# Output products split in two and new engine orders in the RWKV-7 stage of a two-block model on one core

## The reference, cut to what matters

```
def step(state, inp):                       # per head; state is 64 x 64
    r_t, w_t, k_t, v_t, kk_t, a_t = inp
    sa = einsum("bhvk,bhk->bhv", state, -kk_t)
    state = state * w_t + sa * (kk_t * a_t) + v_t * k_t
    y = einsum("bhvk,bhk->bhv", state, r_t)
# then, per head: y = (y - mean(y)) * rsqrt(var(y) + eps); * lnx_w + lnx_b; + bonus; * g
```

## Time and profile before

| | |
|---|---|
| median of three runs | 1938.07 us |
| profiled execution, its own time | 1937.32 us |
| its span, first to last instruction | 1935.4 us |
| PE busy | 1908.9 us, 99% |
| PE weight loads (PEld) busy | 1646.4 us, 85% |
| DVE (VectorE) busy | 1356.2 us, 70% |
| ACT (ScalarE) busy | 847.8 us, 44% |
| mean granted TensorE clock | 0.998 |

### The profile page before, as it was taken

The page is one execution under the profiler, slowest core; times in us unless marked ns, Lnnn a source line. Parts: engine busy times, 40 slices in busy tenths (PEclk is TensorE's granted clock), DMA queues, the critical chain, the costliest instruction groups (busy, mean ns, idle before and its releaser), DMA issues.

```text
span 1935.4 us, 31929 instructions
## 1 busy us (share of the span) xinstructions
PE 1908.9 (99%) x13562; PEld 1646.4 (85%) x13562; DVE 1356.2 (70%) x1796; ACT 847.8 (44%) x1272; POOL 120.9 (6%) x130
## 2 busy tenths in 40 slices
PE   8999999999999999999999999999999999999998
PEld 7877897888788898887989889889887778898897
DVE  7776868576677777667545687767677768777665
ACT  5443744354354334344224454434445645334342
POOL 0155100000000000010000000000002300000000
PEclk9999999999999999999999999999999999999999
DMA  7322402237123233224220132323342113233231
GB/s 241 119 66 66 137 9 90 77 132 131 44 96 101 92 105 110 88 86 135 88 87 23 65 105 94 108 88 109 109 138 87 50 50 103 93 104 110 87 109 45
DMA packets 138829, 182.58 MB, mean 94 GB/s; under 512 B 4917, under 2 KB 103429, under 8 KB 138304
## 3 DMA queue, kind: packets, MB, share of 16 engines
q1 hardware_dynamic: 135392, 168.91, 26.7%
q0 software_dynamic: 3296, 11.63, 2.9%
HBM read 172.66 MB, written 7.34 MB: 93 GB/s over the span
## 4 chain that ended last, share of the span: by engine, by line
PE 94%; DVE 3%; ACT 1%; issue 1%; DMA 0%; DVEq 0%; ACTq 0%
PE X L1680 21%; PE M L1592 19%; PE M L1593 19%; PE M L1594 18%; PE X L713 2%; PE M L1653 1%; PE M L1655 1%; PE M L1654 1%; PE M L2015 1%; PE X L1992 1%; PE X L2003 1%; PE X L1870 1%; DVE w_lo L2519 1%; PE X L1832 0%; PE M L700 0%
## 5 line engine op out<-in xcount | busy, mean ns | idle before, releaser
L1593 PE MATMUL M<-u,raw_lo 128*128 128x512 f32 x728 | 287.9, 396 | 0.0
L1592 PE MATMUL M<-u,w_hi 128*128 128x512 f32 x728 | 287.9, 395 | 0.0
L1594 PE MATMUL M<-u,w_hi 128*128 128x512 f32 x728 | 286.1, 393 | 0.0
L2170 ACT ACTIVATE us<-X 128x256 f32<-128x256 f32 x160 | 61.7, 386 | 433.3 <-PE X L1680 433.2
L2111 ACT ACTIVATE w_hi<-raw 128x2048 fp32r<-128x2048 f32 x111 | 211.7, 1907 | 76.4 <-PE M L1594 42.9
L2677 DVE TENSOR_TENSOR h<-h,M 128x512 f32<-128x512 f32 x184 | 123.6, 684 | 144.9 <-PE M L1594 144.7
L1680 PE MATMUL X<-t,w_hi 128*128 128x256 f32 x936 | 173.2, 282 | 0.0
L1594 PEld LDWEIGHTS M<-u,w_hi 128*128 128x128 f32 x728 | 137.7, 189 | 32.9
L1592 PEld LDWEIGHTS M<-u,w_hi 128*128 128x128 f32 x728 | 136.8, 188 | 30.8
L1593 PEld LDWEIGHTS M<-u,raw_lo 128*128 128x128 f32 x728 | 136.7, 188 | 29.8
L2519 DVE TENSOR_TENSOR raw_lo<-raw,w_hi 128x2048 fp32r<-128x2048 f32 x57 | 130.3, 2286 | 23.7 <-ACT w_hi L2111 23.7
(11 more groups left out here) (561 smaller groups left out, 4581.9 us busy)
## 6 DMA issues: line engine op xcount, KB each, us to landing
raw<-in_w_up_dram SPq DMA_DIRECT2D x48, 1024.0 KB, 5.3
raw<-in_w_down_dram SPq DMA_DIRECT2D x48, 1024.0 KB, 5.1
raw<-in_w_in_dram SPq DMA_DIRECT2D x12, 1024.0 KB, 7.3
raw<-in_a_w_in_dram SPq DMA_DIRECT2D x12, 1024.0 KB, 5.2
h<-in_x_dram SPq DMA_DIRECT2D x16, 256.0 KB, 4.1
raw<-in_w_mk_dram SPq DMA_DIRECT2D x4, 1024.0 KB, 5.1
raw<-in_w_mv_dram SPq DMA_DIRECT2D x4, 1024.0 KB, 5.3
raw<-in_w_out_dram SPq DMA_DIRECT2D x4, 1024.0 KB, 5.1
```

The costliest lines, as they stand in the source:

```text
L1592: mm(dst, wh, xh, start=start, stop=False)
L1593: mm(dst, wl, xh, start=False, stop=False)
L1594: return mm(dst, wh, xl, start=False, stop=stop)
L2170: nc.scalar.activation(at_, region(n, r), ACT.Copy).then_inc(S["st_snap"], 1)
```

## The change

The output operation is divided: `YA` holds the 64 records inside the chunks, `Y` the 28 records with the states. The wait between the parts becomes a wait for `YA`'s own count, and other operations now stand between the two. `half_done` and its semaphore go. For pairs 1 and 3 the output uses banks 2 and 3 in place of banks 0 and 1. The three lists get new orders, and some operations get other banks. The number and shapes of all instructions stay the same.

```
-RW_QUAD = ("L", "RBT", "AR", "PQ", "WG", "MR", "N", "Y")
+RW_QUAD = ("L", "RBT", "AR", "PQ", "WG", "MR", "N", "YA")
 RW_PE = """...
-    TT6.0.1 Z2.1.2 X.1.3 WG.0.2 TT6.1.0 MR.0.1 WG.1.2 N.0.0 fill.25 S1.0.0 MR.1.1 S2.0.1 N.1.2 S3.0.0 S1.1.1 S4.0.0 S2.1.1
-    fill.26 S5.0.0 S3.1.1 fill.27 S6.0.0 S4.1.1 kk2.3.2 S5.1.0 Y.0.2 S6.1.0
-    Y.1.0 var.0.2 var.1.3 fill.28 tV.2.2 fill.29 fill.30 bonus.2.2 fill.31 gate.0.3 gate.1.0 fill.32 tV.3.1 fill.33 fill.34
-    tKd.2.1 L.2.2 fill.35 tBd.2.1 fill.36 RBT.2.1 P2.2.1 PT2.2.0 AR.2.2 P4.2.1 PQ.2.1 L.3.2 TT3.2.0 P8.2.1
-    tA.2.2 fill.37 tBd.3.0 bonus.3.3 tA.3.0 fill.38 tKd.3.0 fill.39 TT4.2.0 P2.3.1 PT2.3.2 Z.2.0 RBT.3.2 P4.3.1 PQ.3.1
+    TT6.0.1 Z2.1.2 X.1.3 WG.0.2 TT6.1.0 MR.0.1 WG.1.2 N.0.0 MR.1.1 N.1.2 S1.0.0 fill.25 S2.0.0 S1.1.1 fill.26 S3.0.0 S2.1.1
+    fill.27 S4.0.0 S3.1.1 YA.0.2 S5.0.0 S4.1.1 YA.1.1 S6.0.0 S5.1.1 fill.28 S6.1.1 Y.0.2 Y.1.1
+    var.0.1 kk2.3.0 var.1.1 tV.2.1 fill.29 fill.30 bonus.2.4 fill.31 gate.0.0 gate.1.1 fill.32 tV.3.3 fill.33 fill.34
+    tKd.2.3 L.2.2 fill.35 tBd.2.3 fill.36 RBT.2.1 P2.2.1 PT2.2.0 AR.2.2 P4.2.1 PQ.2.1 L.3.2 P8.2.1
+    tA.2.0 TT3.2.2 fill.37 tBd.3.0 bonus.3.3 tA.3.0 fill.38 tKd.3.0 fill.39 TT4.2.0 P2.3.1 PT2.3.2 Z.2.0 RBT.3.2 P4.3.1 PQ.3.1
...
-    MR.2.1 WG.3.2 N.2.0 fill.41 S1.2.0 MR.3.1 S2.2.1 N.3.2 S3.2.0 S1.3.1 S4.2.0 S2.3.1 fill.42 S5.2.0 S3.3.1
-    S6.2.0 S4.3.1 fill.43 S5.3.0 Y.2.1 S6.3.0 fill.44 var.2.0 fill.45 Y.3.0 gate.2.2 var.3.3 fill.46 fill.47 gate.3.2""".split()
+    MR.2.1 WG.3.2 N.2.0 MR.3.1 N.3.2 S1.2.0 fill.41 S2.2.0 S1.3.1 fill.42 S3.2.0 S2.3.1 YA.2.2 S4.2.0 S3.3.1
+    YA.3.1 S5.2.0 S4.3.1 fill.43 S6.2.0 S5.3.1 fill.44 S6.3.1 Y.2.2 Y.3.1 var.2.0 fill.45 gate.2.1 var.3.0 fill.46 fill.47 gate.3.1""".split()
 RW_ACT = """...
-    PT4.1 P8.0 P8.1 sq.3 Z.0 Z.1 Z2.0 X.0 yd.0 Z2.1 tA.1 X.1 W.0 G.0 W.1 N.0 G.1 yd.1 yd.2 N.1 yd.3 w.7 dsq.0 ln.3 dsq.1 rn.3
-    var.0 grs.0 tV.2 var.1 ex.3 neg.2 grs.1 ex.2 inc.2 inc.3 dc.3 tV.3 dec.2 dc.2 tKd.2 neg.3 w.8 tBd.2 dec.3 P2.2 PT2.2 P4.2
+    PT4.1 P8.0 P8.1 sq.3 Z.0 Z.1 Z2.0 X.0 yd.0 Z2.1 tA.1 X.1 W.0 G.0 W.1 G.1 N.0 N.1 yd.1 yd.2 yd.3 w.7 dsq.0 dsq.1 ln.3 rn.3
+    var.0 grs.0 var.1 tV.2 ex.3 neg.2 grs.1 ex.2 inc.2 inc.3 dc.3 tV.3 dec.2 dc.2 tKd.2 neg.3 w.8 tBd.2 dec.3 P2.2 PT2.2 P4.2
...
-    dsq.2 var.2 grs.2 dsq.3 var.3 yr.2 grs.3 w.10 yr.3""".split()
+    dsq.2 dsq.3 var.2 grs.2 var.3 yr.2 grs.3 w.10 yr.3""".split()
 RW_DVE = """...
-    TT6.1 MT.0 RT.0 yd.0 S1.0 S2.0 MT.1 S3.0 RT.1 S1.1 S4.0 S2.1 S5.0 yd.1 S3.1 S6.0 yd.2 S4.1 S5.1 S6.1 w.7 kk2.3 t.2 ev.12
+    TT6.1 MT.0 RT.0 yd.0 MT.1 S1.0 RT.1 S2.0 S1.1 S3.0 S2.1 ev.12 S4.0 S3.1 S5.0 S4.1 S6.0 S5.1 yd.1 S6.1 w.7 yd.2 kk2.3 t.2
...
-    K.2 ev.15 B.2 kmod.3 Kd.2 ev.16 R.2 yc.1 bonus.2 Bd.2 L.2 PT.2 gate.1 RBT.2 A.3 B.3 K.3 RKT.2 Kd.3 rk.3 AKT.2 TT2.2 ev.17
-    Bd.3 TT3.2 L.3 R.3 w.8 PT.3 TT4.2 T4.2 ev.18 ev.19 RBT.3 bonus.3 TT2.3 yr.0 TT5.2 T5.2 TT3.3 AKT.3 TT4.3 TT6.2 T4.3 RKT.3
-    TT5.3 T5.3 TT6.3 MT.2 RT.2 S1.2 S2.2 MT.3 S3.2 RT.3 S1.3 S4.2 S2.3 S5.2 S3.3 S6.2 S4.3 w.9 ev.20 S5.3 S6.3 var.2 yb.2 yc.2
+    K.2 ev.15 B.2 kmod.3 Kd.2 ev.16 bonus.2 R.2 yc.1 Bd.2 L.2 PT.2 gate.1 RBT.2 A.3 B.3 K.3 RKT.2 AKT.2 Kd.3 rk.3 TT2.2 ev.17
+    Bd.3 TT3.2 L.3 R.3 w.8 PT.3 TT4.2 T4.2 bonus.3 ev.18 ev.19 RBT.3 TT2.3 yr.0 TT5.2 T5.2 TT3.3 AKT.3 TT4.3 TT6.2 T4.3 RKT.3
+    TT5.3 T5.3 TT6.3 MT.2 RT.2 MT.3 S1.2 RT.3 S2.2 S1.3 S3.2 S2.3 S4.2 S3.3 S5.2 S4.3 S6.2 S5.3 w.9 ev.20 S6.3 var.2 yb.2 yc.2
...
-        RW_BANKS[_x] = RW_QUAD_SETS[_b] if _x[0] in RW_QUAD else (_b,)
+        RW_BANKS[_x] = RW_BANKS[("YA", _x[1])] if _x[0] == "Y" else RW_QUAD_SETS[_b] if _x[0] in RW_QUAD else (_b,)
...
-    if st == "Y":
+    if st == "YA":
         return [("d", ("var", hp))]
...
     for x in RW_OPS["p"]:
-        if x[0] != "fill":
+        if x[0] == "Y":
+            after[x] = []
+        elif x[0] != "fill":
...
-                         S1=["a.N", "d.MT"], Y=["d.S6", "d.RT", "d.RKT", "a.G"], gate=[], var=["a.dsq"])
+                         S1=["a.N", "d.MT"], YA=["d.RKT", "a.G"], Y=["d.S6", "d.RT"], gate=[], var=["a.dsq"])
...
-                    half_done(last)
+                else:
+                    wait("rw_mm", RW_NO["p"][("YA", hp)])
```

More of the change, by code:

```diff
@@ L187 @@
-    var.0 grs.0 tV.2 var.1 ex.3 neg.2 grs.1 ex.2 inc.2 inc.3 dc.3 tV.3 dec.2 dc.2 tKd.2 neg.3 w.8 tBd.2 dec.3 P2.2 PT2.2 P4.2
-    PT4.2 P8.2 tA.2 tBd.3 tA.3 yr.0 tKd.3 w.9 P2.3 PT2.3 Z.2 P4.3 PT4.3 yr.1 P8.3 Z2.2 X.3 Z.3 X.2 Z2.3 W.2 G.2 W.3 N.2 G.3 N.3
-    dsq.2 var.2 grs.2 dsq.3 var.3 yr.2 grs.3 w.10 yr.3""".split()
+    PT4.1 P8.0 P8.1 sq.3 Z.0 Z.1 Z2.0 X.0 yd.0 Z2.1 tA.1 X.1 W.0 G.0 W.1 G.1 N.0 N.1 yd.1 yd.2 yd.3 w.7 dsq.0 dsq.1 ln.3 rn.3
+    var.0 grs.0 var.1 tV.2 ex.3 neg.2 grs.1 ex.2 inc.2 inc.3 dc.3 tV.3 dec.2 dc.2 tKd.2 neg.3 w.8 tBd.2 dec.3 P2.2 PT2.2 P4.2
@@ L190 @@
+    PT4.2 P8.2 tA.2 tBd.3 tA.3 yr.0 tKd.3 w.9 P2.3 PT2.3 Z.2 P4.3 PT4.3 yr.1 P8.3 Z2.2 X.3 Z.3 X.2 Z2.3 W.2 G.2 W.3 G.3 N.2 N.3
+    dsq.2 dsq.3 var.2 grs.2 var.3 yr.2 grs.3 w.10 yr.3""".split()
 RW_DVE = """cs.0 dl.0 cs.1 t.0 ev.4 t.1 kmod.0 w.2 dl.1 ev.5 csx.0 csx.1 dn.0 kk2.0 kmod.1 w.3 ev.6 kk.0 beta.0 Kd.0 K.0 rk.0 Bd.0 ev.7 Kd.1
@@ L256, in program @@
             da_sq da_ss da_ln da_rstd da_y
-            rw_shift rw_p rw_lora rw_act rw_dve rw_half rw_mm y_hi y_lo
+            rw_shift rw_p rw_lora rw_act rw_dve rw_mm y_hi y_lo
             ms_hi ms_lo ma_score ma_max ma_neg ma_exp ma_rz ma_p ma_tr ma_pt_hi ma_pt_lo ma_pv ma_hi ma_lo
@@ L627, in operand @@
                 return blk(sl(name, hp), hh, cp, cpar)
[L629 to L635, removed]
             def out_of_psum(st, hp):
@@ L718, in rwkv_pe @@
                                   start=True, stop=True)
-                elif st != "Y":
+                elif st == "N":
                     for cp in range(4):
@@ L726, in rwkv_pe @@
                                 last = mm(o_, tmv(2, hp, hh, cp, cpar), tmv(3, hp, hh, cp, cpar), start=False, stop=True)
-                else:
+                elif st == "YA":
                     for cp in range(4):
```

## The result

The changed kernel takes 1944.03 us (median of 7 runs, 1942.56 to 1945.71); the kernel before, beside it, 1938.17 (1937.30 to 1938.66). The ratio is 1.003, 95% interval 1.0019 to 1.0042: 5.9 us slower. The profiled execution is the slowest of the seven, 1945.71 us; its span of 1943.9 is 8.5 us above that of before. Part of this is no effect of the change: `N.0`, the first operation behind which the new order begins, starts at 276.01 us in place of 274.44, because TensorE's first matmul came 0.5 us later and about 1 us more was lost before 76 us of the span. I therefore measure one stretch in every profile, from the start of `N.0` to the second matmul of the output projection behind the lists: 109.3 us before (274.44 to 383.76), 116.3 us after (276.01 to 392.27), so 6.9 more. The lines of the changed kernel are numbered 5 or 6 lower than those of before.

The account below looks back on a forecast made before the run. TensorE, busy 99%, was taken as the bound, with only 6.6 us of its waits at stake. Savings and added waits over six steps summed to +1.6 us on the median of 1938.07, so 1939.7 us, range 1936.9 to 1942.3.

Parts of the forecast that it names:

- Step 2: First stand: var.1 in its new bank waits for ScalarE 2.9 us, then tV.2 0.85; 3.7 us added.
- Step 5: States of pairs 2 and 3: 2.0 us saved, then 3.2 added as fill.44 waits for VectorE (second stand).
- rival (a): TensorE's clock falls behind the stands: 1941.3 us for one fall, 1942.9 for two; chance 0.20.
- Step 1: Pairs 0 and 1, up to var.0: waits at state steps, var and inside Y go, about 2.2 us saved.
- Step 3: Gates: gate.1 moves to a free bank and no longer waits for VectorE, 0.9 to 1.0 us saved.
- Step 4: Pairs 2 and 3 before their states: PQ.3 starts 0.4 to 0.5 us earlier, whatever happened before; 0.4 saved.
- Step 6: Tail: fill.46 waits 0.95 us for the bank that ev.21 empties; 0.8 us added.
- Rival (b): Stands smaller than read, TensorE runs into VectorE at L.2 and PQ.3: 1935.4 to 1937.5 us; chance 0.10.
- Rival (c): A wait priced at zero among the P, TT and Z products: 1940.5 to 1941.5 us; chance 0.10.

Follow-up runs that it names:

- e8: Changed kernel with both long TensorE waits mended and VectorE's yd.1, yd.2, w.7 moved into gaps, then the 3.1 us wait at fill.44 put back: 1940.04 us.
- e9: Same as e8, but w.9 and ev.20 two steps earlier on VectorE, so the wait at fill.44 is 1.2 us: 1936.20 us.
- e4: As e1, with w.9 and ev.20 moved two steps earlier on VectorE to shorten the wait at fill.44: 1938.89 us.
- e1: Changed kernel with kk2.3 earlier on TensorE and VectorE, var.1 in bank 0, ScalarE's var.0 ahead of rn.3, removing the first stand: 1942.49 us.
- e2: Changed kernel with VectorE's ev.20 ahead of S4.2 and w.9 behind S6.3, removing the second stand at fill.44: 1939.25 us.
- e3: Changed kernel with the mends of e1 and e2 together, and VectorE's ev.21 ahead of w.9 and var.2: 1936.92 us.
- e6: Kernel before with only the output divided into YA and Y, old orders and old banks: 1937.64 us.
- e5: As e2, plus ScalarE's var.0 ahead of ln.3 and rn.3; banks and TensorE's order as in the changed kernel: 1937.16 us.

## Why the prediction was wrong

The predicted 1939.7 us and the upper end of 1942.3 both lie below 1944.03.

The step that failed is the price of the two stands: steps 2 and 5 charge their length alone, and the sum puts what the clock does behind them at nothing. The falls stand only in rival (a), at a chance of 0.20, and two of them at 0.10, with 1.5 to 1.9 us for each. The profile shows both falls, and the mean clock of 0.995 or 0.996 says the same of all 7 executions. They are worth, by rows of the changed profile: 1.0 us more in `var.1`, 1.0 in `tV.2` and 0.6 to 0.7 in the first seven matmuls of `fill.29`, 2.6 in all, for the first; and for the second 1.7 us, half of the 3.4 us at the low level, all of them work (378.4 to 381.8 us). Between e8 and e9 the part of the 3.8 that isn't length is 1.9 us. Even rival (a) with two falls, 1942.9, would have been 1.1 us too low: a second term that the sum had at nothing is the two waits put down to "issue", 1.7 us. I had the earlier trace rows in hand, and with it a fall after a wait of 1.4 us, 0.7 of work and nothing more. I set against it that steady work follows the stands. That argument didn't hold: in three of the six falls the clock is down before the work begins, and in the other three it falls 0.5 to 1.3 us into steady work (rows in the last section). Either way the work pays. The page "TensorE: Matmul & The Clock Gate" of the Trainium skill, section "HAM oscillation — how this bites in real kernels", warns of such falls; its example has waits of about 3 to 5 us, with the work behind each starting cold. The windows here agree that a wait brings a fall, already after 2.2 to 3.1 us, but in three of six the work started at the full clock. The waits of 1.2 us in e4 and e9 left the clock at 1.00.

Point by point (the list of waits before holds eleven in the stretch, not ten; their sum of 5.8 us is right):

- Step 1: right. The waits of 0.8, 0.2, 0.3 and 0.4 are gone. `var.0` starts 16.2 us after `N.0`; forecast were 15.6. The 0.6 between is a wait of 0.9 us inside `MR.1` put down to "issue". Five of the nine experiments have one there too, of 0.3 to 0.6 us; e1, e2, e3 and e6 have none.
- Step 2: the mechanism and both sizes were right, 2.77 and 0.78 us against 2.9 and 0.85. e5 shows that ScalarE's order, not the bank alone, makes the first of them; with both in place the wait only moves.
- Step 3: right, the 0.9 wait at `gate.1` is gone.
- Step 4: `PQ.3` waits 0.6 for the mask of `RBT.3` as forecast. It was to come 0.4 us early and came 2.45 late, counted from `N.0`: the low clock's 2.6 and the 0.9 in `MR.1`, less what `L.2` (0.2 against 0.6) gave back. So "whatever happened before" was wrong: VectorE was no fixed floor. From 290 to 322 us it is busy for 31.3 us before and 28.9 in the changed kernel, as it waits for TensorE behind the stand, and it comes late with it.
- Step 5: right, 3.14 against 3.2, then the clock.
- Step 6: right, 0.97 against 0.95.
- Rival (b): VectorE's limit was real. Without the stands TensorE does run into VectorE (e1, e3), but from `fill.30` on, 14 us ahead of `L.2`, and for 3.5 us in all; at `L.2` itself it is the 0.5 that was forecast.
- Rival (c), a wait priced at zero, came together with (a): the two "issue" waits of 0.9 and 0.8 us are new against before. One or two of them, at L707 or L700, 0.3 to 0.9 us each, are in the stretch of every kernel with the new orders, and none is in that of before and of e6, which have the old ones. Their cause is open and they were not tested by themselves.

Sum for the stretch: 1.6 forecast, 2.6 and 1.7 for the clock, 1.7 for the "issue" waits, less 0.4 at `L.2`: 7.2, measured 6.9. How much of the 5.9 us between the medians is "issue" waits stays open.

## What to carry to other kernels

Price a stand of TensorE like those here (2.2 to 3.1 us) with the clock: count the matmuls in the 3.4 to 6.8 us behind the fall at double duration, and make that the main case. When operations are moved in several in-order queues, look for two patterns: a bank's reader that stands behind an operation that needs a later product, and a long operation (here 2.3 us) ahead of the one that empties a bank. Before a stand is called the loss, ask which engine would hold TensorE without it: here VectorE took back half of the first one. Where two orders are compared, compare their "issue" waits as well: here they moved by up to 1.2 us without being meant to.

## What the runs showed of the hardware that was not expected

- In the profiles of the changed kernel, e1, e2, e5 and e8 the clock fell in six places in this stretch, inside or just behind waits of 2.2 us (e5), 2.8 (changed, e2) and 3.1 (changed, e1, e8). The waits of 1.2 and 1.3 us in e1, e3, e4 and e9 left it alone. The windows of PE in which it fell, in this order: the changed kernel at `var.1` and at `fill.44`, e1 at `fill.44`, e2 at `var.1`, e5 at `tV.2`, e8 at `fill.44`:

```profile
296.00:297.00 1.00, 0.04 (x1) 0.75 0.00 0
378.00:379.00 1.00, 1.00 (x4) 0.71 0.00 1
375.00:376.00 1.00, 1.00 (x9) 0.58 0.65 194
296.00:297.00 1.00, 0.37 (x1) 0.58 0.00 0
296.00:297.00 1.00, 0.54 (x4) 0.98 0.00 0
370.00:371.00 1.00, 0.00 (x0) 0.76 0.00 0
```

- TensorE starts again at 296.96, 377.95, 373.90, 296.63, 296.46 and 371.88 us. The share that a window lacks to 1.00 puts the falls at 296.5, 378.4, 375.2, 296.2, 297.0 and 370.5 us. So three came inside the wait, and three 0.5 to 1.3 us after its end, in full work. Behind the three falls inside the wait the clock stayed low for 6.8 us each, behind the other three for 3.4 us each: the same wait of 3.1 us gave 3.4 us of low clock in the changed kernel and in e1, and 6.8 in e8. What decides between the two no run shows.
